# A first unit on the unnormed stream, and waits moved between the experts' passes

## The chip, the core and the metric

The kernel runs on one core of a Trainium2 chip. The metric is the device time of one execution in microseconds (us), as the median of the runs shown. The core has four engines that compute: TensorE (PE, with its weight loads PEld), VectorE (DVE), ScalarE (ACT) and GpSimd (POOL). SyncE (SP) only issues DMAs here. Each engine runs its own list of instructions in order; semaphores tie the lists together.

## The reference

Two transformer blocks are computed for 256 tokens of width 1024. The first puts 16 meta tokens ahead (272 rows in all) and begins like this:

```python
n = _rmsnorm(h, pre_mix_norm[l])
proj = jnp.einsum('btd,dn->btn', n, w_in[l])
qkv = jax.nn.silu(_causal_conv(jnp.concatenate([q, k, v], axis=-1), conv_w))
```

where `_rmsnorm` multiplies each row by its own factor `rsqrt(mean(x*x) + EPS)` and by a gain for each column. After that come a gated delta rule, an indexed attention, a gated merge, and a feed-forward layer. The second block has attention over a context, a Fourier branch, and a mixture of 16 experts in 4 groups:

```python
def expert_step(acc, xs):
    w1e, w3e, w2e, ge = xs
    y = (jax.nn.silu(t @ w1e) * (t @ w3e)) @ w2e
    return acc + ge[:, None] * y, None
```

A router picks one group and two experts in it for each token; the other gates are zero. The result is normed once more.

## The kernel before, in words

**Weights.** All weights come as one stream of 1 MB units, each 1024 x 256. A ring of six slots (`ring`) takes them in the order of use; SP issues a slot's next unit when PE has used the one in it. Activations lie transposed, as eight blocks of 128 columns by 272 or 256 tokens.

**Split units.** Most units are multiplied in three parts of reduced-precision fp32: ACT copies the unit rounded into `w_high` (`highs`, L1629), DVE subtracts that copy from the unit and leaves the rest in the slot itself as `ring_low` (`lows`, L2101), and PE adds high x high (L706), high x rest (L707) and low x high (L712). PE waits for `high_ready` at the start of a unit and for `low_ready` ahead of L712. A few units are plain fp32 (`tiles_of_unit`, L679): the very first, ("gk", 0), is one of them.

**The start.** SP fetches the stream into `qc`, then the small constants `sm`, then the ring. ACT squares the stream into `vc` (L1643), PE sums the squares with a matmul of ones (L759), ACT takes the root, DVE the reciprocal `rB` (L2082) and then `nT` = stream x gain x `rB` (L2114). Unit 0 multiplies `nT`. ACT rounds `nT` into `nT_high` (L1650), DVE leaves `nT_rest` (L2120); unit 1 and all later ones of this stage use these two.

**The convolution behind the first twelve units.** Each unit gives two tiles of 128 columns, one to a PSUM bank. For a tile ACT writes the first tap (L1663), DVE adds three more (L2134), ACT takes a sigmoid into `scr` (L1669), POOL multiplies. ACT's list puts the next `w_high` between the sigmoids of a unit's two tiles, and DVE's list puts the next `ring_low` behind the taps of both. ACT then squares finished tiles into `mod_rows` (L1659), and PE sums those (L771) behind every unit from the third on.

**The router.** The product of `h2` (eight blocks, made by DVE from the units of `wo2`) with 20 router columns is a group of fp32 matmuls (L1316); sums of squares (L1324) go to the same bank. Blocks 0 to 5 are multiplied halfway through the last unit of `wo2`, blocks 6 and 7 behind it.

**The experts.** A pass takes two experts, twelve units: eight for the hidden layer (`half_rows`, L1374, the two experts side by side in PE's columns), four for the way back. Eight passes cover 16 experts with up to 64 tokens each; a loop of extra passes, counted at run time (one here), takes what is over, with six units. Twelve more slots (`more`) hold expert weights beside the ring. In a pass PE first gathers tokens for a later pass in some cases (L1386), multiplies, adds the pass before into the accumulators (`scatter`, L1406, from `yb_high` and `yb_low`), turns the hidden rows (L1443), turns the choices and gates (L1447, L668), and multiplies back (L1374 on `hid`; L1418 in the extra pass). ACT empties the turned hidden rows (`hid`, L2040), then the turned choices (`spread`), then the gates (`gate_slot`, L2045); DVE leaves the low half of the output rows (`yb_low`, L2756). Behind the loop come the last `scatter`, the residual (L2866), the squares' sum (L1481) and the norm.

The order of the work is written out by hand; nothing plans it.

Of the kernel before, what the change touches and what calls it, by code (L numbers as in the profile page):

```python
# [9 lines left out]
KT = D // 128  # L10
META = 16
SEQ = 256
T = META + SEQ
# [114 lines left out]
STAGGER = 16  # L128
# [44 lines left out]
def build(nc, stream, h_in, ctx_in, c1_in, c2_in, sm_in, ws_in, wr_in, lam_in, out):  # L173
# [4 lines left out]
    with top:  # L178
# [52 lines left out]
        with ExitStack() as mixer:  # L231
# [33 lines left out]
            with ExitStack() as m:  # L265
# [74 lines left out]
        with ExitStack() as m:  # L340
# [25 lines left out]
            _under_merged2 = sb(m, "under_merged2", 128, 2 * KT * UNIT_COLS + 2 * KT * SEQ + STAGGER - 272 - used_words)  # L366
# [24 lines left out]
        h2tok_ready, h2tok_low_ready = sem("h2tok_ready"), sem("h2tok_low_ready")  # L391
# [84 lines left out]
        nT_rest_ready = sem("nT_rest_ready")  # L476
        cleared_ready = sem("cleared_ready")
# [38 lines left out]
        rexp_ready = sem("rexp_ready")  # L516
# [34 lines left out]

        CONV_TILES = [(kind, j) for kind in ("gk", "gq", "gv") for j in range(H)]
# [88 lines left out]
        def _(pe):  # L641
# [54 lines left out]
            def split_tiles(kind, u, high_x, low_x, n, names, k_ready=lambda k: None, halfway=lambda: None, drains=1):  # L696
# [4 lines left out]
                for k in range(KT):  # L701
                    k_ready(k)
                    for j in range(2):
# [69 lines left out]
            for t in range(0, 24, 2):  # L773
# [534 lines left out]
            def router_blocks(blocks):  # L1308
# [9 lines left out]
                if blocks[0] == 0:  # L1318
                    pe.wait_ge(partial_ready, 3)
                for k in blocks[-1:] if blocks[0] == 0 else blocks:  # L1320
# [16 lines left out]
            def between_wo2(u):  # L1337
# [3 lines left out]
                elif u == 3:  # L1341
                    router_blocks(range(6))

            pe.wait_ge(small_loaded, 32)
            for u in range(4):
                split_tiles("wo2", u, lambda k: merged2_high[:, k, :], lambda k: merged2_low[:, k, :], SEQ, [("wo2", u)],
                            lambda k: pe.wait_ge(merged2_ready, k // 2 + 1) if u == 0 else None, lambda: between_wo2(u), drains=0)
            router_blocks(range(6, KT))
            pe.wait_ge(h_ready, 3 * KT)
# [1687 lines left out]
```

## Time and profile before

| | |
|---|---|
| median of 3 runs | 1209.31 us (1208.77 to 1213.37) |
| the profiled execution | 1205.35 us, of which the span is 1203.2 us |
| PE busy | 1153.4 us, 96% of the span |
| DVE, ACT, POOL busy | 663.2, 499.2, 87.0 us |
| DMA | 254.59 MB, mean 212 GB/s; 420 to 422 GB/s through most of the experts' passes |

The page's engine rows tell how long each engine was busy; PE's ends are modelled, so a busy PE is not PE at its peak. What counts for an edit is the stage that it touches: which wait ends last there. The timeline lists instructions with the idle time ahead of each and what ended it; the chain of waits follows the end of the execution back to its start; the waits view sums who waited for whom.

### The profile page before, as it was taken

What the parts mean: (1) busy time and instruction counts of PE and PEld (TensorE: products, weight loads), DVE (VectorE), ACT (ScalarE), POOL (GpSimd) and SP (SyncE); (2) the same over time, 40 slices, a digit from 0 to 9 for tenths busy, and PEclk for the clock granted to TensorE, in tenths of its full rate; (3) what the DMA queues carried; (4) which work ended last, traced back from release to release, by engine and by line L of the source; (5) the groups of instructions that cost most, each with busy time, mean ns of one, the idle gap of its engine ahead of it and who ended that gap; (6) DMA issues with size and microseconds to landing.
All of it is one profiled execution on the core that took longest, in us unless ns stands there. A gap on an engine that the chain in (4) does not pass through costs nothing.

```text
span 1203.2 us, 21401 instructions
## 1 busy us (share of the span) xinstructions
PE 1153.4 (96%) x8936; PEld 996.9 (83%) x8936; DVE 663.2 (55%) x1143; ACT 499.2 (41%) x797; POOL 87.0 (7%) x92
## 2 busy tenths in 40 slices
PE   7999899999999989999999999999999899999996
PEld 6998789998979969999979889767899766665764
DVE  5777875588866476665555342775557531221223
ACT  5766523644374555544445222667344311111112
POOL 2451320000000100000100000000002000000000
PEclk9999999999999999999999999999999899999998
DMA  9544240443514746555564321302857899999980
GB/s 368 206 143 175 71 176 1 141 154 131 189 54 152 270 176 245 189 196 184 202 245 175 116 94 71 141 2 114 340 181 299 335 422 421 420 420 420 422 366 36
DMA packets 36204, 254.59 MB, mean 212 GB/s; under 512 B 4048, under 2 KB 4192, under 8 KB 5904
## 3 DMA queue, kind: packets, MB, share of 16 engines
q1 hardware_dynamic: 33552, 237.84, 51.4%
q0 software_dynamic: 2560, 15.42, 3.3%
q8 instruction: 71, 1.16, 0.4%
q14 instruction: 21, 0.17, 0.0%
HBM read 252.19 MB, written 1.05 MB: 210 GB/s over the span
## 4 chain that ended last, share of the span: by engine, by line
PE 85%; DVE 9%; ACT 3%; issue 2%; DMA 0%; DVEq 0%; ACTq 0%
PE bank L1374 13%; PE bank L712 12%; PE bank L706 12%; PE bank L707 12%; PE bank L668 5%; PE bank L1096 5%; PE bank L1182 4%; PE bank L1103 3%; PE bank L1386 2%; PE bank L759 2%; PE bank L1406 2%; PE bank L728 1%; PE bank L883 1%; DVE ring_low L2101 1%; PE bank L1284 1%
## 5 line engine op out<-in xcount | busy, mean ns | idle before, releaser
L2101 DVE TENSOR_TENSOR ring_low<-ring,w_high 128x2048 fp32r<-128x2048 f32 x104 | 238.0, 2290 | 160.8 <-ACT w_high L1629 160.7
L1629 ACT ACTIVATE w_high<-ring 128x2048 fp32r<-128x2048 f32 x104 | 199.1, 1915 | 281.5 <-PE bank L712 192.9
L706 PE MATMUL bank<-nT_high,w_high 128*128 128x256 f32 (+1 forms) x448 | 114.6, 295 | 0.0
L706 PEld LDWEIGHTS bank<-nT_high,w_high 128*128 128x128 f32 x448 | 84.2, 188 | 2.6 <-issue 2.4
L1374 PE MATMUL bank<-more,xs 128*64 128x256 f32 x768 | 84.6, 379 | 0.0
L1374 PEld LDWEIGHTS bank<-more,xs 128*64 128x64 f32 x768 | 58.7, 137 | 25.7 <-issue 2.2
L706 PE MATMUL bank<-hcl,w_high 128*128 128x256 f32 (+1 forms) x272 | 73.1, 306 | 0.0
L707 PE MATMUL bank<-hcl,w_high 128*128 128x256 f32 (+1 forms) x272 | 71.2, 299 | 0.0
L707 PE MATMUL bank<-nT_low,w_high 128*128 128x256 f32 (+1 forms) x272 | 64.7, 280 | 0.0
L706 PE MATMUL bank<-nMs,w_high 128*128 128x256 f32 x256 | 60.3, 280 | 1.4 <-DVE nMs L2493 1.4
L1096 PE MATMUL bank<-up,w_high 128*128 128x256 f32 x512 | 60.7, 276 | 0.0
L712 PE MATMUL bank<-nT_high,ring_low 128*128 128x256 f32 (+1 forms) x448 | 59.0, 284 | 0.5 <-DVE ring_low L2101 0.5
L707 PE MATMUL bank<-nMs,w_high 128*128 128x256 f32 x256 | 59.4, 276 | 0.0
L1096 PEld LDWEIGHTS bank<-up,w_high 128*128 128x128 f32 x512 | 59.3, 188 | 0.0
L712 PEld LDWEIGHTS bank<-nT_high,ring_low 128*128 128x128 f32 x448 | 55.8, 188 | 1.2 <-DVE ring_low L2101 0.7
L706 PEld LDWEIGHTS bank<-hcl,w_high 128*128 128x128 f32 x272 | 51.2, 188 | 4.1 <-issue 2.1
L707 PEld LDWEIGHTS bank<-hcl,w_high 128*128 128x128 f32 x272 | 51.2, 188 | 3.1 <-issue 1.0
L707 PEld LDWEIGHTS bank<-nT_low,w_high 128*128 128x128 f32 x272 | 51.2, 188 | 1.5 <-issue 1.4
L2756 DVE SCALAR_TENSOR_TENSOR yb_low<-bank,gate_slot,yb_high 128x512 fp32r<-128x512 f32 x18 | 13.5, 751 | 69.7 <-ACT yb_high L2049 69.7
L706 PEld LDWEIGHTS bank<-nMs,w_high 128*128 128x128 f32 x256 | 48.1, 188 | 3.0 <-issue 1.8
L707 PEld LDWEIGHTS bank<-nMs,w_high 128*128 128x128 f32 x256 | 48.1, 188 | 0.0
L707 PE MATMUL bank<-nT_rest,w_high 128*128 128x272 f32 x176 | 44.4, 288 | 0.0
(565 smaller groups left out, 2479.5 us busy)
## 6 DMA issues: line engine op xcount, KB each, us to landing
ring<-stream SPq DMA_DIRECT2D x163, 1024.0 KB, 4.9
more<-stream SPq DMA_DIRECT2D x60, 1024.0 KB, 18.7
more<-stream POOLq DMA_DIRECT2D x10, 1024.0 KB, 15.0
c<-constants_one SPq DMA_DIRECT2D x1, 1657.0 KB, 16.2
qc<-h_in SPq DMA_DIRECT2D x4, 272.0 KB, 3.8
c<-constants_two POOLq DMA_DIRECT2D x1, 1056.0 KB, 9.0
beside<-stream POOLq DMA_DIRECT2D x1, 1024.0 KB, 13.0
hT<-h_in POOLq DMA_DIRECT2D x1, 1024.0 KB, 6.0
```

The source lines that it names most:

```text
L668: last = nc.tensor.matmul(dst, lhs, rhs, start=(i == 0), stop=(i == len(pairs) - 1))
L706: nc.tensor.matmul(into[j], w, high_x(k), start=first, stop=False, skip_group_check=True)
L707: nc.tensor.matmul(into[j], w, low_x(k), start=False, stop=False, skip_group_check=True)
L712: last = nc.tensor.matmul(into[j], low_w[:, k, j * 128:(j + 1) * 128], high_x(k), start=False, stop=(k == KT - 1), skip_group_check=True)
L759: last = nc.tensor.matmul(psum[banks.at[name]][:, 0:n], ones, src[:, k, :], start=(k == 0), stop=(k == KT - 1), skip_group_check=True)
L1096: nc.tensor.matmul(dst[:, j * SEQ:(j + 1) * SEQ], high_w[:, k, j * 128:(j + 1) * 128], up[:, kg * KT + k, part, :], start=(kg == 0 and k = ...
L1103: last = nc.tensor.matmul(dst[:, j * SEQ:(j + 1) * SEQ], low_w[:, k, j * 128:(j + 1) * 128], up[:, kg * KT + k, 0, :], start=False, stop=( ...
L1182: return nc.tensor.matmul(dst[tp][:, j * 256:(j + 1) * 256], hcl[:, 2 * tp + part, k, j * 128:(j + 1) * 128], w[:, k, :], start=first, sto ...
L1374: last = nc.tensor.matmul(dst[rows, :], stationary[:, k, rows], w[j][:, k, :], start=(k == 0), stop=(k == n_k - 1))
L1386: last = nc.tensor.matmul(dst, part[:, qt, ft * 128:(ft + 1) * 128], pick[:, qt, 0:width], start=(qt == 0 and part is h2tok_high), stop=(q ...
L1629: A(w_high[:, d % 2, :], ring[:, s, :], ACT.Copy).then_inc(high_ready, 1)
L2101: TT(ring_low[:, s, :], ring[:, s, :], w_high[:, d % 2, :], sub).then_inc(low_ready, 1)
```

## The change

- **Start.** DVE multiplies the stream by the gain alone into `gained` (eight operations, in the room of `sums`) as soon as the stream has landed. Unit 0 multiplies `gained` instead of `nT`, so it needs no root. DVE multiplies its two output banks by `rB` in place, behind `nT_rest` and ahead of the first `ring_low`; ACT's first two taps wait for that. ACT makes the first `w_high` ahead of `nT_high`. Unit 1 waits for `nT_rest` block by block.
- **Router.** Blocks 0 to 5 are multiplied among the blocks of the last `wo2` unit; only the squares stay halfway.
- **Experts.** The first pass turns the choices ahead of the hidden rows. Every pass waits for `gate_slot` ahead of the second half of the way back, not of the first. `scatter` waits for each half of `yb_low` by itself. In an extra pass half of the `scatter` goes ahead of `half_rows` and half behind, and the wait for the gates goes down to where they are used.
- **Names and places.** One semaphore is shared to make room for the new one; `STAGGER` goes from 16 to 48 words, which moves buffers by 32 or more words.

```diff
-STAGGER = 16
+STAGGER = 48
...
+                _stagger_dsa = sb(m, "stagger_dsa", 128, STAGGER)
...
-            _under_merged2 = sb(m, "under_merged2", 128, 2 * KT * UNIT_COLS + 2 * KT * SEQ + STAGGER - 272 - used_words)
+            _under_merged2 = sb(m, "under_merged2", 128, 2 * KT * UNIT_COLS + 2 * KT * SEQ + STAGGER + 16 - 272 - used_words)
...
+        gained = sums[:, 0:H * T].rearrange("p (k n) -> p k n", n=T)
...
                 if t == 0:
-                    tiles_of_unit(kind, u, nT, T, names, k_ready=lambda k: pe.wait_ge(nT_ready, k + 1))
+                    tiles_of_unit(kind, u, gained, T, names, k_ready=lambda k: pe.wait_ge(gained_ready, k + 1))
                 else:
-                    if t == 2:
-                        pe.wait_ge(nT_rest_ready, KT)
-                    split_tiles(kind, u, lambda k: nT_high[:, k, :], lambda k: nT_rest[:, k, :], T, names)
+                    split_tiles(kind, u, lambda k: nT_high[:, k, :], lambda k: nT_rest[:, k, :], T, names,
+                                lambda k: pe.wait_ge(nT_rest_ready, k + 1) if t == 2 else None)
...
                 elif u == 3:
-                    router_blocks(range(6))
+                    router_squares([5])
+
+            def among_wo2(u, k):
+
+                blocks = {0: [0], 1: [1], 2: [2], 3: [3], 5: [4], 7: [5]}.get(k)
+                if u == 3 and blocks:
+                    router_blocks(blocks)
...
-            def scatter(count, signal=False, first=False):
-
-                pe.wait_ge(ys_ready, count * 2 + 2)
-                pe.wait_ge(spread_ready, count + 1)
-                for ft in range(KT):
+            def scatter(count, signal=False, first=False, fts=range(KT)):
+
+                if fts[0] == 0:
+                    pe.wait_ge(spread_ready, count + 1)
+                for ft in fts:
+                    if ft % 4 == 0:
+                        pe.wait_ge(ys_ready, count * 2 + 1 + ft // 4)
...
                     gather_blocks(range(KT), 2 * CAP)
-                    scatter(count - 1)
+                    scatter(count - 1, fts=range(4))
...
+                if first:
+                    turn_choices()
+                    turn_hidden()
+                else:
+                    scatter(count - 1, first=(n == 1), fts=range(KT) if n < PAIRS else range(4, KT))
+                    turn_hidden()
+                    turn_choices()
...
-                pe.wait_ge(gate_slot_ready, count * 2 + 2)
                 for q in range(2):
+                    if q == 1:
+                        pe.wait_ge(gate_slot_ready, count * 2 + 2)
...
             with pe.Fori(0, extra) as x:
-                pe.wait_ge(gates_loaded, 2 * x + 2)
                 expert_pass(PAIRS, x, x + PAIRS, lambda qt: gate_of[:, qt, :])
...
+            highs(1)
             for k in range(KT):
                 act.wait_ge(nT_ready, k + 1)
                 A(nT_high[:, k, :], nT[:, k, :], ACT.Copy).then_inc(nT_high_ready, 1)
-            highs(1)
...
             def tap(t):
                 kind, j = CONV_TILES[t]
+                if t < 2:
+                    act.wait_ge(gained_ready, KT + t + 1)
...
             dve.wait_ge(sm_loaded, 16)
+            for k in range(KT):
+                dve.wait_ge(h_loaded[k // 2], 16)
+                TS(gained[:, k, :], qc[:, k, :], small("g_pre_mix")[:, k:k + 1], None, mul).then_inc(gained_ready, 1)
             inv_rms("ss_in", T)
...
+            for t in range(2):
+                bank = full(dve, CONV_TILES[t])
+                TT(bank[:, 0:T], bank[:, 0:T], rB[:, 0:T], mul).then_inc(gained_ready, 1)
             lows(1)
```

DVE's list at the start of the program, before, from the reciprocal of the root to the first `ring_low`:

```order
L2082 RECIPROCAL rB<-root 128x272 [waits bank_free0,sm_loaded]
L2114 SCALAR_TENSOR_TENSOR nT<-qc,sm,rB 128x272 [waits dve_step]
L2114 SCALAR_TENSOR_TENSOR nT<-qc,sm,rB 128x272 x7
L2116 TENSOR_TENSOR silu_c<-sm,a 128x8x2 [waits sig_ready]
L2120 TENSOR_TENSOR nT_rest<-nT,nT_high 128x272 [waits nT_high_ready] x8
L2101 TENSOR_TENSOR ring_low<-ring,w_high 128x2048 [waits high_ready]
```

The same place after, where `sums` is the room of `gained` and `unit_used0` stands for the second tile of unit 0:

```order
L2146 TENSOR_SCALAR sums<-qc,sm 128x272 [waits h_loaded0,sm_loaded]
L2146 TENSOR_SCALAR sums<-qc,sm 128x272 [waits h_loaded0]
L2146 TENSOR_SCALAR sums<-qc,sm 128x272 [waits h_loaded1] x2
L2146 TENSOR_SCALAR sums<-qc,sm 128x272 [waits h_loaded2] x2
L2146 TENSOR_SCALAR sums<-qc,sm 128x272 [waits h_loaded3] x2
L2114 RECIPROCAL rB<-root 128x272 [waits bank_free0]
L2149 SCALAR_TENSOR_TENSOR nT<-qc,sm,rB 128x272 [waits dve_step]
L2149 SCALAR_TENSOR_TENSOR nT<-qc,sm,rB 128x272 x7
L2151 TENSOR_TENSOR silu_c<-sm,a 128x8x2 [waits sig_ready]
L2155 TENSOR_TENSOR nT_rest<-nT,nT_high 128x272 [waits nT_high_ready] x8
L2158 TENSOR_TENSOR bank<-bank,rB 128x272 [waits bank_full1]
L2158 TENSOR_TENSOR bank<-bank,rB 128x272 [waits unit_used0]
```

Eight operations stand ahead of the reciprocal now, and two on banks stand between `nT_rest` and the first `ring_low`, which comes next.

PE's list at the end of the eighth pass and the entry of the loop of extra passes, before (`more,hid` is the way back, `c` holds the identity, `plan` the count of extra passes, `pick` the gather):

```order
L1447 MATMUL bank<-c,pick_again 128x128 [waits again_ready]
L1447 MATMUL bank<-c,pick_again 128x128
L668 MATMUL bank<-c,pick_again 128x2 x2
L1374 MATMUL bank<-more,hid 64x512 [waits more_loaded2,more_loaded5,gate_slot_ready,hid_ready]
L1374 MATMUL bank<-more,hid 64x512 x7
L1374 MATMUL bank<-more,hid 64x512 [waits more_loaded7,more_loaded6]
L1374 MATMUL bank<-more,hid 64x512 x7
L634 TENSOR_LOAD plan [waits plan_ready]
L634 ISA x2
L1473 UNCONDITIONAL_BRANCH
L1473 ISA
L1434 ISA [waits gates_loaded]
```

The same place after, down to the first matmul of the gather:

```order
L1467 MATMUL bank<-c,pick_again 128x128 [waits again_ready]
L1467 MATMUL bank<-c,pick_again 128x128
L671 MATMUL bank<-c,pick_again 128x2 x2
L1388 MATMUL bank<-more,hid 64x512 [waits more_loaded5,more_loaded2,hid_ready]
L1388 MATMUL bank<-more,hid 64x512 x7
L1388 MATMUL bank<-more,hid 64x512 [waits more_loaded7,more_loaded6,gate_slot_ready]
L1388 MATMUL bank<-more,hid 64x512 x7
L637 TENSOR_LOAD plan [waits plan_ready]
L637 ISA x2
L1504 UNCONDITIONAL_BRANCH
L1504 ISA
L1400 MATMUL bank<-pick,c_rounded 128x128 [waits pick_ready]
```

The wait for `gate_slot_ready` went down by eight matmuls, and the wait for `gates_loaded` left the head of the loop.

## Rows read from the trace of the kernel before

**Rows 1.** The page: shares of the chain that ended last, by engine

```profile
PE 85%; DVE 9%; ACT 3%; issue 2%; DMA 0%; DVEq 0%; ACTq 0%
```

**Rows 2.** Timeline of the start: start us, length us, engine, line, operation, count, idle before

```profile
4.38 6.89 PE L759 MATMUL bank<-vc,ones 128*128 128x272 f32 x16 [4.38 <-ACT vc L1643]
...
14.44 8.96 PE L679 MATMUL bank<-nT,ring 128*128 128x272 f32 x32 [3.17 <-DVE nT L2114]
...
17.18 2.90 DVE L2120 TENSOR_TENSOR nT_rest<-nT,nT_high 128x272 fp32r<-128x272 f32 x8
...
20.00 2.29 DVE L2101 TENSOR_TENSOR ring_low<-ring,w_high 128x2048 fp32r<-128x2048 f32 x1
...
24.14 1.91 ACT L1629 ACTIVATE w_high<-ring 128x2048 fp32r<-128x2048 f32 x1
...
29.00 3.04 DVE L2134 SCALAR_TENSOR_TENSOR kc<-bank,sm,kc 128x271 f32<-128x271 f32 x6 [0.63 <-ACT kc L1663]
...
33.08 0.74 ACT L1659 ACTIVATE mod_rows<-kc 128x272 f32<-128x272 f32 x2
...
35.22 1.08 PE L771 MATMUL bank<-mod_rows,ones 128*128 128x272 f32 x4
```

**Rows 3.** One tile's instructions, `nT`: count, ns min/median/max, first and last start

```profile
L2114 DVE SCALAR_TENSOR_TENSOR nT<-qc,sm,rB x8: 497/498/502, 13.8 to 16.7; 128x272 f32<-128x272 f32 x8
```

**Rows 4.** DVE's groups by shape: count, busy us, mean ns, idle before

```profile
L2361 DVE TENSOR_TENSOR rot<-bank,c 128x272 f32<-128x272 f32 x3 | 1.3, 440 | 0.9 <-PE bank L978 0.8
```

**Rows 5.** DMA issues at 2.6 and 3.1 us: count, KB, us to landing

```profile
sm<-smalls SPq DMA_DIRECT2D x1, 127.0 KB, 4.7
ring<-stream SPq DMA_DIRECT2D x1, 1024.0 KB, 7.1
```

**Rows 6.** PE's timeline in the last unit of wo2

```profile
934.10 2.75 PE L1316 MATMUL bank<-wr,c 128*128 128x20 f32 x24
```

**Rows 7.** PE's waits after 900 us: total us, times, longest us

```profile
PE bank L1374 <- ACT hid L2040: 3.0, 4, 0.8
PE bank L1386 <- DVE gate_of L2858: 1.8, 1, 1.8
...
PE bank L1406 <- DVE yb_low L2756: 1.6, 1, 1.6
PE bank L1443 <- DVE hid_rows L2787: 1.4, 2, 0.9
...
PE bank L1418 <- ACT gate_slot L2045: 0.8, 1, 0.8
```

**Rows 8.** The chain in the experts' passes: start us, length us, what

```profile
969.59 0.22 PE bank L1447 x2
969.81 0.34 PE bank L668 x4
...
998.36 0.68 issue
...
1128.73 3.63 PE bank L1386 x32
...
1153.19 2.07 PE bank L1406 x16
...
1165.90 5.62 PE bank L1386 x32
...
1174.80 7.11 PE bank L1374 x64
```

**Rows 9.** DVE's timeline at its entry of the loop of extra passes

```profile
1155.20 0.15 DVE L2849 COPY shift<-c 128x1 f32 x1 [1.18 <-issue]
```

**Rows 10.** Busy us by PE, PEld, DVE, ACT, POOL, then granted clock, DMA share, GB/s

```profile
1170.00:1171.00 1.00, 1.00 (x7) 1.00 (x7) 0.00 (x0) 0.00 (x0) 0.00 (x0) 0.50 0.29 123
```

**Rows 11.** The DMA issued at 1121.3 us: count, KB, us to landing

```profile
more<-stream SPq DMA_DIRECT2D x1, 1024.0 KB, 26.1
```

**Rows 12.** PE's timeline in the eighth pass

```profile
1146.11 7.08 PE L1374 MATMUL bank<-more,xs 128*64 128x256 f32 x64
```

More of the change, by code:

```diff
@@ L702, in split_tiles @@
                     k_ready(k)
+                    among(k)
                     for j in range(2):
@@ L1317, in router_blocks, with router_squares @@
                                          start=(k == 0 and qt == 0), stop=False, skip_group_check=True)
-                if blocks[0] == 0:
-                    pe.wait_ge(partial_ready, 3)
-                for k in blocks[-1:] if blocks[0] == 0 else blocks:
+            def router_squares(blocks):
+                dst = psum[banks.at["router"]]
+                pe.wait_ge(partial_ready, 3)
+                for k in blocks:
                     if k >= 6:
@@ L1346, in _ @@
                 split_tiles("wo2", u, lambda k: merged2_high[:, k, :], lambda k: merged2_low[:, k, :], SEQ, [("wo2", u)],
-                            lambda k: pe.wait_ge(merged2_ready, k // 2 + 1) if u == 0 else None, lambda: between_wo2(u), drains=0)
+                            lambda k: pe.wait_ge(merged2_ready, k // 2 + 1) if u == 0 else None, lambda: between_wo2(u), drains=0,
+                            among=lambda k: among_wo2(u, k))
             router_blocks(range(6, KT))
+            router_squares(range(6, KT))
             pe.wait_ge(h_ready, 3 * KT)
@@ L1435, in expert_pass, with turn_hidden, turn_choices @@
                     gather_blocks(range(KT), 2 * CAP)
-                    scatter(count - 1)
+                    scatter(count - 1, fts=range(4))
                     for q in range(2):
                         half_rows(n, again, 2 * q, psum[q][:, 0:256], xs[:, :, 0:2 * CAP], KT, UNIT_COLS, rows_ready if q == 0 else lambda k: None)
-                if n < PAIRS and not first:
-                    scatter(count - 1, first=(n == 1))
-                pe.wait_ge(hid_rows_ready, count + 1)
-                for k in range(4 if n < PAIRS else 2):
-                    last = nc.tensor.transpose(psum[2][:, k * 128:(k + 1) * 128], hid_rows[:, k * 128:(k + 1) * 128], ident)
-                last.then_inc(hid_full, 1)
-                pe.wait_ge(again_ready, count * 4 + 4)
-                for qt in range(2):
-                    nc.tensor.transpose(psum[3][:, qt * 128:(qt + 1) * 128], pick_again[:, qt, :], ident)
-                group(psum[3][:, SEQ:SEQ + 2], [(pick_again[:, qt, :], gates(qt)) for qt in range(2)]).then_inc(spread_full, 1)
+                def turn_hidden():
+                    pe.wait_ge(hid_rows_ready, count + 1)
+                    for k in range(4 if n < PAIRS else 2):
+                        last = nc.tensor.transpose(psum[2][:, k * 128:(k + 1) * 128], hid_rows[:, k * 128:(k + 1) * 128], ident)
+                    last.then_inc(hid_full, 1)
+                def turn_choices():
+                    pe.wait_ge(again_ready, count * 4 + 4)
+                    for qt in range(2):
+                        nc.tensor.transpose(psum[3][:, qt * 128:(qt + 1) * 128], pick_again[:, qt, :], ident)
+                    if n == PAIRS:
+                        pe.wait_ge(gates_loaded, 2 * again + 2)
+                    group(psum[3][:, SEQ:SEQ + 2], [(pick_again[:, qt, :], gates(qt)) for qt in range(2)]).then_inc(spread_full, 1)
+                if first:
[5 more added lines that the diff above has]
+                    turn_choices()
                 if n == 0:
```

17 lines of the change are left out of this document (9 added, 8 removed).

## The prediction

> **What bounds the kernel now.** I read the chain by engine first: PE carries 85% of it, DVE 9%, DMA nothing [rows 1]. So a gain must be time in which PE stands still or runs slowly, and it counts only if nothing else ends late in its place. Then the timeline of the start: PE sums squares from 4.38 to 11.27, stands 3.17 us until the first `nT`, and multiplies unit 0 from 14.44 to 23.40 [rows 2]. Last PE's waits in the experts' part: four of about 0.75 us for `hid`, 1.8 us for the gates of the extra pass, 1.6 us for `yb_low`, 0.9 us for the first hidden rows, 0.8 us for `gate_slot` [rows 7]. The change goes at each of these. [...]
>
> **The start.** `gained` needs `sm`, which lands at 2.59 + 4.7 = 7.3 us, and slot 0, at 3.06 + 7.1 = 10.2 us [rows 5]. I price its eight operations at no more than 0.5 us each, by an operation of the same size with one more operand [rows 3]; that fills 4 us of DVE's idle time and is done by 11.3 us. So unit 0 starts at 11.3 instead of 14.44 and ends by 20.3 even at the old 8.96 us. That is 3.1 us on PE, but I don't take it, because what is late next is DVE and ACT. `nT_rest` still ends at 20.0 [rows 2]: the reciprocal and `nT` have not moved, and making `w_high` first costs `nT_high` nothing that DVE sees, since DVE's eight are the slower. Then come the two new operations on banks. No row shows DVE writing a bank; reading one at this size costs 0.44 us [rows 4], so I take 0.9 us for both, with ends of 0 (hidden) and 1.8 us (twice the row). Queued behind them on DVE: `ring_low`, the taps of the first tile, then ACT's sigmoid and its next `w_high`. That `w_high` ended at 24.14 + 1.91 = 26.05; now 26.95. PE gets there earlier: two units take 35.22 - 23.40 = 11.8 us, 5.9 each, so unit 1 ends by 26.2, and PE starts unit 2 at 27.0 instead of some 29.3. Then `ring_low` of unit 2 ends at 29.25, the taps behind it start there instead of at 29.00, so ACT's squares end at 33.08 + 0.74 + 0.25 = 34.07 instead of 33.82. PE, back from unit 2 at about 33, waits for them at L771: its second half goes at 34.2 instead of 35.22 + 0.5 = 35.7. From there DVE and ACT gain on PE in each unit, since in the trace they stand idle before every set of taps. So the start is worth **1.5 us**, and with the ends above 0.7 to 2.4. It barely hangs on how fast unit 0 runs. All that comes later starts from PE, and moves with it.
>
> **The router.** The same 24 matmul records of 128x20 move by some microseconds, from one block to six pieces. Together they take 2.75 us, 0.11 each, whatever their few columns [rows 6]; cut in six they hide at most partly behind wide matmuls. I take 0, with a loss of up to 0.6 (0.1 for each return) and a gain of as much. The wait behind the unit, for DVE's last `h2`, stays.
>
> **The passes.** In the first, the turned choices take 0.22 + 0.34 = 0.56 us [rows 8] and now lie within the 0.9 us that PE waits for the hidden rows: **0.56**. In passes two, four, six and eight PE starts the way back 0.68 us after `hid` is done [rows 8], because it waits for `gate_slot`, three operations further in ACT's list; I leave 0.09 for the signal, so 4 x 0.59 = **2.36**. The moved wait stands ahead of the second half, eight matmuls later, when ACT's short operations on the gates are over; what is queued behind it is that half alone. In the other passes a gather lies there already: 0.
>
> **The extra pass.** PE started the gather at 1165.90 [rows 8] after standing 1.8 us [rows 7], so it is done with the eighth pass at 1164.1. With the gates' wait gone, what remains is the entry of the loop: loading the count and a branch. No row shows it alone on PE. DVE stood 1.18 us at its own entry [rows 9], with one load more; the other end is 0, hidden while the last matmuls run. I take 0.6. [...]
>
> So: gather from 1164.7 at the full clock, 3.63 to 1168.3; half a `scatter`, 2.07 / 2 = 1.04 [rows 8], to 1169.4; `half_rows` 7.11 to 1176.5; the other half of `scatter`, 1.04, to 1177.5, half of it beside DVE's making of the hidden rows. The turn came at 1174.80 + 7.11 + 0.5 = 1182.4 before: **4.9 us**, of which 1.2 are the wait, 3.2 the clock and 0.5 the overlap. Then `gate_slot`, 0.8 less 0.1: **0.7**. At the last `scatter` PE waits 1.6 us for the second `yb_low`, while the first is done before the multiplication ends; half the `scatter`, **1.0**, goes into that. DVE's residual starts as much earlier, so the squares' sum is not held up.
>
> **Sum.** 1.5 + 0 + 0.56 + 2.36 + 4.9 + 0.7 + 1.0 = 11.0 us. The profiled execution took 1205.35 us and would take 1194.3; against the median, 1209.31 - 11.0 = **1198.3 us**. The ends of the unknown prices give 8 to 13.5 us, 1195.8 to 1201.3.
>
> **The rivals.**
>
> *The clock stays down in the extra pass.* If the loop's entry costs PE all of DVE's 1.18 us, the gap shrinks only from 1.8 to 1.2, and the granted clock may fall as before: 0.6 + 3.2 less, 7.2 us gained, 1202.1. For it: the fall behind the gap of 1.8. Against it: the gaps of 0.75 in four passes have no slow matmuls behind them. [...] Chance 0.15.
>
> *The stream of weights becomes the bound.* Through the passes the DMAs are full, whatever PE does. A unit for the last quarter of the eighth pass's hidden layer was issued at 1121.3 and landed 26.1 us later, at 1147.4 [rows 11]; PE takes it in the second half of the 7.08 us from 1146.11, at 1149.6 [rows 12]. So 2.2 us are left, and by then PE is 0.56 + 3 x 0.59 = 2.3 us ahead. It fits only just. If the stream lands later by some us, PE waits there, and the 2.9 us of the passes go: 8.1 gained, 1201.2. Chance 0.10.
>
> *The start gives nothing.* If the two bank operations cost several times the row, or PE's new short waits there (about 0.8 us at unit 2, 1.2 at L771) bring the lower clock, the 1.5 go: 1199.8. Chance 0.10.
>
> *Slower.* `STAGGER` moves buffers by 32 words or more. If PE read its operands more slowly at the new addresses, its whole share of the chain would stretch, 0.85 x 1203.2 = 1023 us [rows 1]. From 1.7% on that is 17.4 us, more than the 11 gained and the 6 that a measurement can tell: 1215.7. Against it: eight operations on rows of 272 words, at eight different offsets, agree within 497 to 502 ns [rows 3]. Chance 0.03.
>
> *It doesn't do what it says*: waits merely trade places and all lies within 6 us. Chance 0.02.
>
> **How the numbers follow.** The forecast has 0.60. Forecast, clock, stream and start are faster by over 0.5%, about what a measurement here can tell from no change (below 1203.3): 0.95 less some for two of them at once and for the spread of the runs, 0.88. Within it 0.09, slower 0.03. The range takes the forecast's own 1195.8 to 1201.3, the clock and the stream up to 1202.1, and two rivals together up to 1204.5; below, an us for the spread: 1194.5 to 1204.5.
>
> **What would show it.** Right: L679 begins at about 11.3, PE idles before unit 2, and L771's second half begins near 34.2; the way back in even-numbered passes starts 0.1 us after `hid`; the gather of the extra pass takes 3.6 us at granted clock 1.00 and `half_rows` starts 4.7 us after the eighth pass. Wrong: bank operations over 1 us each, a wait for a DMA in passes seven to nine, a granted clock of 0.50 behind the eighth pass, or longer steps between matmuls everywhere.

## The result and the profile after

The changed kernel takes 1190.03 us (median of four executions, 1189.76 to 1190.30), the kernel before 1210.34 us measured beside it (1208.77 to 1213.37). The ratio is 0.983, with a 95% interval of 0.981 to 0.985: 20.3 us gained, where 11.0 were forecast and 1194.5 us was the lower end of the range. The direction and every place at which the forecast saw a gain were right; the size was not. One execution of the experiment on the gates ran at a mean granted clock of 0.841 and took 1307.34 us; it is in no median below.

The profiled execution of the changed kernel took 1190.30 us, with a span of 1188.5 us at a mean granted clock of 0.995. The one of before took 1205.35 us, 1203.2 and 0.988. So the two traces show 15 us, and another 5 us lie between the profiled execution of before and its own median. Both parts need an explanation. (In all that follows a *fall* of the clock is a stretch at a granted clock of 0.50, the lowest in the 18 traces; outside the falls they show 1.00.)

First the timeline of the start (start, length, engine, line; L759 of before is L763 now, L679 is L682, L771 is L775), which answers to [rows 2]:

```profile
4.23 6.83 PE L763 MATMUL bank<-vc,ones 128*128 128x272 f32 x16 [4.23 <-ACT vc L1673]
6.93 2.26 DVE L2146 TENSOR_SCALAR sums<-qc,sm 128x272 f32<-128x272 f32 x8 [5.58 <-DMA sm<-smalls]
10.90 7.50 PE L682 MATMUL bank<-sums,ring 128*128 128x272 f32 x32
...
19.72 0.79 DVE L2158 TENSOR_TENSOR bank<-bank,rB 128x272 f32<-128x272 f32 x2
...
24.55 1.90 ACT L1659 ACTIVATE w_high<-ring 128x2048 fp32r<-128x2048 f32 x1
...
33.21 1.18 PE L775 MATMUL bank<-mod_rows,ones 128*128 128x272 f32 x4 [0.39 <-ACT mod_rows L1689]
```

PE goes from the squares' sum to unit 0 without standing still; `sums` is the tile that holds `gained`. Unit 0 takes 7.50 us instead of 8.96, DVE's two operations on the banks 0.79 us together. L775 begins 2.0 us before L771 did.

Then the same timeline in the extra pass: the end of the eighth pass's way back, the first two matmuls of the gather, its last, and the scatter and hidden rows behind it. It answers to [rows 8] and [rows 10].

```profile
1152.63 4.03 PE L1388 MATMUL bank<-more,hid 128*64 128x512 f32 x18
1156.59 0.33 PE L1400 MATMUL bank<-pick,c_rounded 128*128 128x128 f32 x1
1156.75 0.27 PE L1400 MATMUL bank<-pick,h2tok_low 128*128 128x128 f32 x1
...
1160.10 0.28 PE L1400 MATMUL bank<-pick,h2tok_low 128*128 128x128 f32 x1
1160.21 0.34 PE L1422 MATMUL bank<-spread,yb_high 128*128 128x256 f32 x1
...
1161.30 7.13 PE L1388 MATMUL bank<-more,xs 128*64 128x256 f32 x64
```

No gap is left: the way back ends at 1152.63 + 4.03 = 1156.66 and the gather has begun at 1156.59. It takes 1160.38 - 1156.59 = 3.8 us instead of 5.62, and the stretches around it have a granted clock of 1.00 (PE's busy time is the first pair of numbers, the clock the number before the DMA share):

```profile
core 0: us, PE busy (x) PEld busy (x) DVE busy (x) ACT busy (x) POOL busy (x), PEclk, DMA share, GB/s
141.00:144.00 3.00, 2.59 (x13) 2.33 (x14) 2.91 (x4) 0.63 (x3) 1.81 (x2) 1.00 0.89 295
144.00:147.00 3.00, 2.75 (x15) 2.15 (x14) 2.83 (x10) 0.28 (x1) 0.41 (x1) 1.00 0.45 188
165.00:168.00 3.00, 2.63 (x22) 2.62 (x23) 1.69 (x3) 1.11 (x2) 1.42 (x2) 1.00 1.02 431
168.00:171.00 3.00, 3.00 (x29) 3.00 (x28) 1.38 (x2) 0.68 (x2) 1.45 (x2) 1.00 1.03 437
1160.00:1170.00 10.00, 10.00 (x91) 7.32 (x90) 1.53 (x3) 0.57 (x2) 0.00 (x0) 1.00 0.26 109
...
```

In the trace of before two stretches between 140 and 175 us, which the forecast didn't look at, have a granted clock of 0.51 and 0.53:

```profile
144.00:147.00 3.00, 3.00 (x9) 2.38 (x8) 2.90 (x4) 0.00 (x0) 0.64 (x2) 0.51 0.80 311
168.00:171.00 3.00, 3.00 (x17) 3.00 (x16) 0.37 (x2) 1.10 (x2) 1.61 (x2) 0.53 1.02 431
```

Last, the waits of PE that answer to [rows 7] (engine, what it works on, who is waited for: total, times, longest). Those for `hid`, `gate_of` and `gate_slot` are gone, the one for `yb_low` fell from 1.6 to 0.4, the one for the hidden rows from 0.9 to 0.2; new are 1.6 and 0.4 us at the start.

```profile
PE bank L710 <- ACT w_high L1659: 1.6, 1, 1.6
PE bank L1422 <- DVE yb_low L2794: 0.4, 1, 0.4
PE bank L775 <- ACT mod_rows L1689: 0.4, 1, 0.4
PE bank L1460 <- DVE hid_rows L2825: 0.2, 1, 0.2
```

Where the 14.7 us between the two spans arise, by how much earlier the same line of PE starts in the trace of after:

| up to | gained so far | in this stage | forecast |
|---|---|---|---|
| end of the start (L771, L775 and on to 140 us) | 1.8 us | 1.8 | 1.5 |
| 200 us | 3.1 | 1.3 | no term |
| head of the experts' part, 940 us, the router with it | 4.2 | 1.1 | 0 |
| way back of the first pass | 4.9 | 0.7 | 0.56 |
| end of the eighth pass | 7.4 | 2.5 | 2.36 |
| turn in the extra pass | 13.1 | 5.7 | 4.9 |
| way back of the extra pass | 13.9 | 0.8 | 0.7 |
| end | 14.7 | 0.8 | 1.0 |

So the stages that the forecast named give 12.3 us against 11.0 in this pair of traces. What it had no term for is 2.4 us within the traces and 5 us outside them.

### The profile page after: what moved, and what is told of

Its sections match the earlier page's. It is cut to its first block, busy times and chain, and to the rows that moved or that the text cites. A ratio compares the mean times of both kernels' runs of the same rounds, so it can differ in the third digit from the quotient of the medians.

```text
span 1188.5 us, 21411 instructions
## 1 busy us (share of the span) xinstructions
PE 1145.3 (96%) x8936; PEld 981.5 (83%) x8936; DVE 665.7 (56%) x1153; ACT 497.4 (42%) x797; POOL 86.2 (7%) x92
## 4 chain that ended last, share of the span: by engine, by line
PE 85%; DVE 9%; ACT 3%; issue 2%; DVEq 0%; ACTq 0%
PE bank L1388 15%; PE bank L716 12%; PE bank L710 12%; PE bank L711 12%; PE bank L671 5%; PE bank L1099 5%; PE bank L1185 4%; PE bank L1106 3%; PE bank L1400 2%; PE bank L1422 1%; PE bank L732 1%; DVE ring_low L2133 1%; PE bank L886 1%; PE bank L763 1%; PE bank L1211 1%
## 5 line engine op out<-in xcount | busy, mean ns | idle before, releaser
L1388 PEld LDWEIGHTS bank<-more,xs 128*64 128x64 f32 x768 | 55.0, 137 | 29.3 <-issue 2.3
```

The lines of the kernel that those rows point to most:

```text
L1388: last = nc.tensor.matmul(dst[rows, :], stationary[:, k, rows], w[j][:, k, :], start=(k == 0), stop=(k == n_k - 1))
```

## The experiments

**Is before's median another kernel than its profile?** The kernel before, unchanged, was run again with a second trace, and so were the start alone, everything but the start, and the shift of the buffers alone. I had two theories of the missing part: the granted clock falls at other places in other executions (clock theory), or the matmuls run faster at the new addresses (address theory).

> The kernel before, unchanged. Its profiled execution took 1205.35 us at a mean granted clock of 0.988, its other executions 1208.77 to 1213.37 us. Clock theory: what differs between executions is how often and where the granted clock falls to half, since an idle stretch such as the ones at 141 to 144 and 165 to 168 us is followed by slow matmuls in some executions and not in others; so the times spread over 1205 to 1213 us again, a longer execution has a lower mean clock (about 0.98 at 1210 us), and a second trace shows falls at other places than 13.8, 144, 168, 942, 949 and 1167 us. Address theory (the shifted buffers speed up what follows): the mean clock is 0.988 whatever the time, and the falls lie where they lay.

Measured: 1209.76 us, ratio 1.000 (0.998 to 1.002). Neither theory held alone. Over this study the kernel before was executed 98 times beside the others, in four sets. At a mean clock of 0.987 there are 38 different times: 7 between 1204.4 and 1205.4 us, 31 between 1209.3 and 1212.1, and none between. So the same program at the same clock has two times, 3.9 us apart at the nearest and some 5 us by their middles, and besides, times go with the clock (1202.6 to 1203.3 us at 0.989 and 0.990, 1206.4 to 1208.0 for nearly all at 0.985). How many fall into the faster group changes: none of the 98 lies between 1208.0 and 1209.0 us, and below that lie 6 of 29, 10 of 23, 18 of 24 and 6 of 22 of the four sets, whose medians are 1210.16, 1209.33, 1207.33 and 1209.73 us. So a kernel is best read against the executions of before in its own set. The changed kernel was measured in one set only, ahead of these four, and a distance of 2 or 3 us between it and a kernel of another set tells little. The profiled execution of before belonged to the faster group, its median to the slower one. The second trace belongs to the slower, and shows what the difference is. These rows give the shortest, middle and longest duration in ns and the first and last start of one line's matmuls; first the kernel before as profiled, then its second trace:

```profile
L706 PE MATMUL bank<-nMs,w_high x256: 276/276/392, 438.3 to 528.3; 128*128 128x256 f32 x128
L1096 PE MATMUL bank<-up,w_high x512: 276/276/285, 530.4 to 616.6; 128*128 128x256 f32 x171
```

```profile
L706 PE MATMUL bank<-nMs,w_high x256: 277/279/392, 435.5 to 527.8; 128*128 128x256 f32 x128
L1096 PE MATMUL bank<-up,w_high x512: 279/279/284, 529.9 to 618.6; 128*128 128x256 f32 x171
```

The stretch over `nMs` takes 92.3 us instead of 90.0, that over `up` 88.7 instead of 86.2: 4.8 us. A profiled duration overlaps the next matmul and its end is modelled, so the firmer figure is the step, the time from the start of one of them to the start of the next: in the middle it is 118 ns instead of 113. Its mean, without pauses, is 117.8 to 118.4 ns in the second trace and 113.6 to 116.2 in the first, whether ACT, DVE, both or neither are busy. So the longer step doesn't come from those engines being busy. Below, 276 ns stands for the short step and 279 ns or more for the longer one.

**The shift alone.**

```diff
-STAGGER = 16
+STAGGER = 48
+                _stagger_dsa = sb(m, "stagger_dsa", 128, STAGGER)
-  ... 2 * KT * SEQ + STAGGER - 272 - used_words)
+  ... 2 * KT * SEQ + STAGGER + 16 - 272 - used_words)
```

> The kernel before with only the buffers moved, by 32 words and more. Address theory: 4 us or more of the gain that no term of the forecast covers, 1206 us or less beside 1210.3, and the gain grows evenly from 290 to 920 us. Clock and price theories: the same time as the kernel before within 2 us, and the same lengths of the matmuls between 290 and 920 us.

Measured: 1203.43 us, ratio 0.995 (0.993 to 0.997), 6.7 us at the median; its 12 executions lie between 1201.27 and 1205.46 us, in one group. Over `nMs` and `up` the matmuls take 276 ns, without exception in the five traces with 48 words in this place:

```profile
L1097 PE MATMUL bank<-up,w_high x512: 276/276/280, 527.9 to 613.8; 128*128 128x256 f32 x171
```

The change of constants that the forecast priced at nothing is, with the extra pass, the largest single term. Against the trace of before, which had the short step as well, it still gains 1.4 us between 290 and 940 us, most of it outside that stage: 0.9 us lie between 859 and 933 us, in the matmuls over `hcl` and their neighbours. This is most of the 1.1 us in the table's third row.

**The shift taken out of the changed kernel**, the same edit backwards:

> The changed kernel with the addresses of the kernel before. Address theory: the matmuls over nMs and up between 438 and 616 us go back to some 279 to 280 ns instead of 276 in most executions, 1500 of them by 3 ns, and the median is 4.7 to 6.7 us above the changed kernel, 1194.7 to 1196.7 us, with some executions at 1190 to 1191 us at the same mean clock. Clock theory: the addresses do nothing in a kernel whose clock falls only twice, 1190 to 1191 us throughout.

Measured: 1195.40 us, ratio 0.990 (0.988 to 0.992), so 5.4 us above the changed kernel, and spread over 1193.37 to 1198.35 again. Its trace fell on the shortest of them, with 276 ns. The clock theory, 1190 to 1191 us throughout, fell. Of the eight traces with the old addresses four have the short step and four the longer one, each in both stretches.

**Which filler?** Only the first one is enlarged, so that `nMs`, `up` and the mixer's buffers move against the weights:

```diff
-        _stagger = sb(dense, "stagger", 128, STAGGER)
+        _stagger = sb(dense, "stagger", 128, 48)
-  ... 2 * KT * SEQ + STAGGER - 272 - used_words)
+  ... 2 * KT * SEQ + 48 - 272 - used_words)
```

> The kernel before, where only the first filler (behind the high parts of the weights) grows from 16 to 48 words; the second and third stay, so nMs, up and the mixer's buffers lie as in the changed kernel relative to the weights, and the buffers behind the other fillers don't. If the relative place of nMs and up is the cause: 1203.4 us beside 1210.2, and 276 ns between 438 and 616 us. If it is one of the other buffers: 1210 us.

Measured: 1206.27 us, ratio 0.998 (0.996 to 0.9995), with 276 ns over `up`. So this filler brings the fast step, as its trace shows. It doesn't bring the whole gain: 3.1 us beside its own runs of before, 6.7 with all fillers. In its trace unit 0 ran at a granted clock of 0.50 from 13 to 20 us, so part of the rest is that. Another part comes with the other fillers: between 859 and 933 us this kernel gains 0.1 us on the trace of before, the one with all fillers 0.9. What more they bring stays open. All these edits move many buffers at once, so they show that places matter, not which operand of a matmul it is.

**Other places.** The changed kernel with fillers of 32, 64, 80, 112 and 40 words; the only edit is the constant, `STAGGER = 32` and so on.

> The changed kernel with fillers of 32 words instead of 48. If each place but the old one is as good (a single unlucky address): 1190 us and 276 ns. If the old place and its neighbours share the loss: 1194.7 us or more, and 279 ns or more between 438 and 616 us.

> The changed kernel with fillers of 64 words. So far 32 words gave 281 ns between 438 and 616 us and 1199.9 us, 16 words 276 in some executions and 280 in others, 48 words 276. If the pattern repeats every 32 words, 64 is like 32: 281 ns and about 1200 us. If it is a matter of distance (further is better): 276 ns and 1190 us or less.

> The changed kernel with fillers of 80 words. Pattern of 32 words: like 16 and 48, 276 ns, 1190 to 1195 us. Distance: 276 ns and no more than 1190 us. If 48 is a lucky place alone: 279 ns or more and 1195 us or more.

> The changed kernel with fillers of 112 words. If the places repeat every 32 words and 16, 48 and 80 are of one kind: 276 or 280 ns by execution, 1190 to 1196 us, and not the 281 ns and 1200 us of 32 and 64. If they repeat every 64 words: like 48, 276 ns and 1190 us in each execution.

> The changed kernel with fillers of 40 words, between the slow 32 and the fast 48. If the time goes gradually with the place: 278 to 279 ns and some 1195 us. If what counts is a block of 16 words that a buffer begins in: as slow as 32, 281 ns and 1200 us, or as fast as 48, 276 ns and 1190 us.

| words | median us | executions | ratio to before (95%) | middle duration over `up` in the trace |
|---|---|---|---|---|
| 16 | 1195.40 | 1193.37 to 1198.35 | 0.990 (0.988 to 0.992) | 276 ns |
| 32 | 1199.91 | 1198.14 to 1200.71 | 0.992 (0.990 to 0.994) | 281 |
| 40 | 1203.29 | 1201.47 to 1204.11 | 0.994 (0.993 to 0.996) | 280 |
| 48 | 1190.03 | 1189.76 to 1190.30 | 0.983 (0.981 to 0.985) | 276 |
| 64 | 1203.32 | 1201.22 to 1205.57 | 0.996 (0.994 to 0.998) | 283 |
| 80 | 1193.71 | 1191.86 to 1198.40 | 0.988 (0.985 to 0.991) | 279 |
| 112 | 1191.36 | 1189.80 to 1193.16 | 0.985 (0.982 to 0.989) | 276 |

The row of 32 words, then that of 64, in the same view as above:

```profile
L1099 PE MATMUL bank<-up,w_high x512: 274/281/287, 530.6 to 619.6; 128*128 128x256 f32 x171
```

```profile
L1099 PE MATMUL bank<-up,w_high x512: 274/283/283, 534.9 to 624.7; 128*128 128x256 f32 x171
```

The step goes with the duration: 113 ns in the middle for 276 ns, 117 to 120 ns for the longer ones. There are three kinds of places. 48 and 112 words had the short step in every trace. 16 words has either step, and so has 80 by its times: at one mean clock, 0.994, two of its executions took 1193.38 and 1197.56 us. 32, 40 and 64 words are the slowest, each in one trace with the longer step. So 48 is not a lucky place alone, more distance is not better, and the time doesn't pass gradually from 32 to 48 (40 is slower than 32, for a reason not found). The seven places would fit a pattern that repeats every 64 words, with 32, 40 and 64 bad; seven places don't prove one. The stage between 859 and 933 us has the same order: against the changed kernel 112 words lose nothing there, 16 and 80 lose 0.8 and 0.9 us, 32, 40 and 64 lose 1.6, 1.8 and 2.1, by one trace each. With 64 words the change of addresses gives away 13 of the 20 us. What the spread of 16 and 80 comes from at unchanged addresses isn't settled: no row of the traces differs ahead of the stage in which the steps do.

**The start.** First alone on the kernel before (its core, the rest as in the change):

```diff
-                    tiles_of_unit(kind, u, nT, T, ... nT_ready ...)
+                    tiles_of_unit(kind, u, gained, T, ... gained_ready ...)
+            for t in range(2):
+                bank = full(dve, CONV_TILES[t])
+                TT(bank[:, 0:T], bank[:, 0:T], rB[:, 0:T], mul)
```

> Only the start of the change: unit 0 on the stream times the gain, the banks scaled by the root, the high parts of the second weight unit first. Price theory (the step of 1.5 us as forecast, 1.8 in the traces): 1208.5 to 1209 us beside 1210.3, and the two falls of the clock near 144 and 168 us stay. Clock theory: a start without the 3.2 us idle stretch also moves the falls near 144 and 168 us, so 3 to 8 us are gained, 1202 to 1207 us, with a mean clock above that of the kernel before. Address theory: 1.8 us and no more.

Measured: 1208.08 us, ratio 0.998 (0.996 to 0.9998), 2.1 us at the median. Its two falls of the clock lie at 140 to 144 and 164 to 168 us, so a better start doesn't remove them. On the time and on these falls the price theory is right. But the mean clock is above before's, as the clock theory had it: 0.987 to 0.991, where before's executions of the same set have 0.983 to 0.989.

Then the change without its start:

> The changed kernel with the start of the kernel before. Price theory: 1190.0 + 1.8 = 1191.8 us. Clock theory: 3 to 8 us more than the changed kernel, 1193 to 1198 us, with falls of the clock back near 144 and 168 us, at half the clock for some 3 us each. Address theory: 1191.8 us, and the falls near 144 and 168 us absent, as in the changed kernel.

Measured: 1193.82 us, ratio 0.986 (0.983 to 0.989), 3.8 us above the changed kernel. None of the three fits: the time is the clock theory's, but there is no fall near 144 or 168 us. Its trace says why it is more than 1.8: the squares' sum, the wait and unit 0, with the clock at 0.50 from 14 to 21 us.

```profile
4.57 6.86 PE L761 MATMUL bank<-vc,ones 128*128 128x272 f32 x16 [4.57 <-ACT vc L1672]
14.61 10.63 PE L680 MATMUL bank<-nT,ring 128*128 128x272 f32 x32 [3.17 <-DVE nT L2143]
```

Unit 0 takes 10.63 us here, 8.96 in the first trace of before and 7.57 in the second. In four of seven traces with the old start the clock fell in unit 0, in three it didn't; in none of the nine with the new start did it fall there. That raised the question what the clock alone is worth there. I filled the wait with matmuls whose sums nothing uses:

```diff
                 if t == 0:
+                    for _ in range(12):
+                        nc.tensor.matmul(psum[banks.turn % 8][:, 0:T], ones, vc[:, 0, :], start=True, stop=True)
                     tiles_of_unit(kind, u, nT, T, names, ...
```

> The kernel before with twelve more matmuls of 128x272 in the 3.2 us in which PE waits for the first nT; their sums are overwritten by unit 0 and used by nothing. If the start's gain beyond the forecast is the clock's (a fall to half in unit 0 in some executions, 0 to 3.6 us): unit 0 takes 7.5 us in the trace, none of the clock's falls lies before 30 us, and the median is 1 to 3 us lower than the kernel before. If the clock doesn't matter there: the same time within 0.5 us, or longer by what the twelve stick out.

Measured: 1205.96 us, ratio 0.998 (0.996 to 1.001): inconclusive. One matmul leaves two records here (the twelve are x24 in the timeline), so the filling took 5.66 us and unit 0 began at 16.14, more than 2 us after it could have. With six (`range(6)`):

> The kernel before with six more matmuls of 128x272 in the wait for the first nT, 12 records of 0.235 us, 2.8 us, so that they don't stick out as the twelve before them did (24 records, 5.66 us, 2.4 us too long). Clock theory of the start: unit 0 begins some 3.2 us after the squares' sum as before and takes 7.5 us in the trace, and the median is 0.5 to 3 us below the kernel before. If the start's gain is the earlier beginning alone: the same time within 0.5 us.

Measured: 1209.84 us, ratio 1.000 (0.998 to 1.002).

```profile
4.38 5.48 PE L759 MATMUL bank<-vc,ones 128*128 128x272 f32 x16 [4.38 <-ACT vc L1645]
9.70 2.91 PE L779 MATMUL bank<-vc,ones 128*128 128x272 f32 x12
13.03 7.57 PE L679 MATMUL bank<-nT,ring 128*128 128x272 f32 x32 [0.42 <-DVE nT L2116]
```

Unit 0 takes 7.57 us at a granted clock of 1.00, as in the twelve-fold filling (7.50 us, 1.00), and the median doesn't move by more than the interval of 2 to 3 us. So the fall in unit 0 is real where it happens, but it isn't what separates the median of before from its profile.

What the start gains the traces show better. These rows are the matmuls over `beside`, the next ones behind the convolution (first and last start at the end), in the first trace of before, in its second, and in the trace of the start alone:

```profile
L668 PE MATMUL bank<-beside,nT x48: 398/399/399, 96.3 to 107.4; 128*128 128x280 f32 x48
```

```profile
L668 PE MATMUL bank<-beside,nT x48: 398/399/399, 93.5 to 104.6; 128*128 128x280 f32 x48
```

```profile
L670 PE MATMUL bank<-beside,nT x48: 398/399/399, 92.9 to 103.9; 128*128 128x280 f32 x48
```

The squares' sum ends between 9.5 and 11.4 us in the traces, so I count from its end to the first of these matmuls: 83.3 to 83.4 us in the nine traces with the new start, 83.7 to 83.8 in the three with the old start and no fall in unit 0, and 85.0 to 86.9 in the four with the fall. The earlier beginning is therefore worth 0.2 to 0.5 us by itself, because DVE and ACT are late next; the rest of what the start gains is the fall that no longer happens. The kernel with six matmuls has no fall there either and comes to 83.7 us, so it should gain nearly as much, and its median doesn't show it. Whether before's executions fall in unit 0 as often as its traces isn't shown; for the median the interval of the start alone allows 0.2 to 5.2 us.

**The gates of the extra pass.** The wait moved, on the kernel before, and nothing else:

```diff
-                pe.wait_ge(gates_loaded, 2 * x + 2)
                 expert_pass(PAIRS, x, x + PAIRS, ...)
 ... in expert_pass, behind the turned choices:
+                if n == PAIRS:
+                    pe.wait_ge(gates_loaded, 2 * again + 2)
```

> The kernel before, where only the wait for the gates of the extra pass moves behind the turned choices. Forecast's step: 1.2 us of wait and 3.2 us of clock, 4.4 us gained; with a loop entry that costs nothing 5.0, so 1205.2 to 1205.8 us beside 1210.2; the gather at 3.6 us and full clock. Rival (the clock stays down behind the eighth pass whatever the wait): 0.6 to 1.8 us gained, 1208.4 to 1209.6 us, the gather at 5.6 us again.

Measured: 1202.74 us, ratio 0.9955 (0.9935 to 0.997), 6.6 us at the median. Against the trace of before PE is 4.6 us late at the end of the eighth pass (this trace has the longer step over `nMs` and `up`) and 0.5 us early behind the extra pass's multiplication: 5.1 us gained there, where 4.4 to 5.0 were expected. Here are the gather's rows of before, of this kernel and of the changed kernel with the wait put back (count, busy us and mean ns, then idle time before them), each from the stretch of 1148 to 1176 us:

```profile
L1386 PE MATMUL bank<-pick,c_rounded 128*128 128x128 f32 x16 | 5.3, 354 | 1.8 <-DVE gate_of L2858 1.8
```

```profile
L1386 PE MATMUL bank<-pick,c_rounded 128*128 128x128 f32 x16 | 3.7, 277 | 0.0
```

```profile
L1400 PE MATMUL bank<-pick,c_rounded 128*128 128x128 f32 x16 | 5.2, 348 | 1.8 <-DVE gate_of L2895 1.8
```

The last one is this experiment, the move undone in the changed kernel:

```diff
-                    if n == PAIRS:
-                        pe.wait_ge(gates_loaded, 2 * again + 2)
 ...
+                pe.wait_ge(gates_loaded, 2 * x + 2)
                 expert_pass(PAIRS, x, x + PAIRS, ...)
```

> The changed kernel with the wait for the gates back at the head of the extra pass. If the gap brings the clock's fall: 1.8 us of wait and some 3.2 us of clock come back, 1195.0 us beside 1190.0, and the gather takes 5.6 us. If the fall of the kernel before came from its earlier gaps: 1.8 us alone, 1191.8 us, and the gather takes 3.7 us.

Measured: 1196.18 us, ratio 0.989 (0.9855 to 0.993), 6.2 us above the changed kernel, 5.1 of them in the extra pass by the traces. The clock falls again behind a gap of 1.8 us:

```profile
1158.00:1161.00 3.00, 1.22 (x6) 0.14 (x2) 0.99 (x5) 0.69 (x1) 0.00 (x0) 1.00 1.00 423
1161.00:1164.00 3.00, 2.95 (x21) 2.96 (x22) 1.24 (x5) 0.00 (x0) 0.00 (x0) 0.80 0.99 418
1164.00:1167.00 3.00, 3.00 (x15) 3.00 (x16) 0.41 (x1) 0.00 (x0) 0.00 (x0) 0.50 0.36 153
```

So the wait cost 1.8 us and its clock 3.3, in both directions of the edit, by one trace each. The fall itself stands behind the eighth pass in all eight traces with the wait at the head of the extra pass, and in none of the ten without it.

**The experts' part alone**, on the start and the addresses of before:

> The kernel before with the experts' part of the change alone (first pass, way back, extra pass, last scatter), addresses and start as before. Forecast's terms: 0.56 + 2.36 + 4.9 + 0.7 + 1.0 = 9.5 us, with a loop entry of 0 us instead of 0.6 some 10.1; 1199.5 to 1200.5 us beside 1210. In the trace the matmuls over nMs and up take 276 ns or 280, as in the kernel before. If the gain of the experts hangs on the addresses or the start as well: under 8 us, 1202 us or more.

Measured: 1196.67 us, ratio 0.991 (0.987 to 0.994), 10.7 us at the median. In its trace PE is 2.2 us late behind the router (the granted clock was 0.50 there from 938 to 948.2 and from 951.8 to 955 us, in the trace of before from 942.2 to 945.7 and from 949.2 to 952.5), and the span ends 8.2 us earlier (1195.0 against 1203.2): 10.4 us, where the terms gave 9.5 to 10.1. The gain of the experts hangs neither on the start nor on the addresses. The three parts measured alone, 2.1, 6.7 and 10.7 us, add up to 19.5 of the 20.3 us; the router's part was not measured alone.

## Why the forecast was wrong

**The start, 1.5 us: right in its steps, lucky in its size.** `gained` was ready in time, unit 0 began at 10.90 (11.3 forecast), the bank operations took 0.40 us each (0.44 by [rows 4]), ACT's `w_high` ended at 26.45 (26.95), and L775's second half went at 33.21 + 1.18 / 2 = 33.8 (34.2). PE's new wait at unit 2 is 1.6 us instead of 0.8, because unit 0 was faster than assumed; what was late next was ACT, as said. 1.8 us came of it. But the sentence "It barely hangs on how fast unit 0 runs" holds for the changed kernel only. In the kernel before L706 starts at 23.0 us or at 20.2, according to the clock in unit 0, and the trace that the forecast was read from had a granted clock of 0.50 from 13.8 to 17.2 us, in part of it. Without that fall the same steps give 0.2 to 0.5 us, with a longer one more than 3.

**The router, 0: right.** The distance between the two traces is 4.3 us ahead of it and 4.2 to 4.3 behind it.

**The passes, 0.56 + 2.36: right**, 0.7 and 2.5. In the even passes PE starts the way back at 1149.57, after ACT's `hid` of 1148.92 and 0.60 us, so 0.05 us behind it; `gate_slot`, until 1150.10, is no longer waited for.

```profile
1148.92 0.60 ACT L2072 ACTIVATE hid<-bank 128x512 f32<-128x512 f32 x1 [8.78 <-PE bank L1460]
1149.48 0.39 ACT L2074 ACTIVATE spread<-bank 128x256 fp32r<-128x256 f32 x1
1149.76 0.34 ACT L2077 ACTIVATE gate_slot<-bank 64x1 f32<-64x1 f32 x2
```

**The extra pass, 4.9 + 0.7 + 1.0: right but for the loop's entry.** The 0.6 us for it were an estimate between DVE's 1.18 us [rows 9] and 0; no row of before shows PE's entry alone. In the trace of after the gather begins at 1156.59 us and the way back ends at 1156.66: PE's entry costs nothing that shows, so 5.7 us came instead of 4.9. The end of the range was the right value. The 3.2 us of clock in the 4.9 are 2.0 us of the gather and 1.2 of the `scatter` behind it, by [rows 8], at the clock of [rows 10]; the two traces of the experiment on the gates' wait put back give 3.3.

**The shift of the buffers, no term: this is the step that failed.** The forecast named `STAGGER` as the one way to a slower kernel, at 0.03, and argued from DVE's rows [rows 3] that addresses don't matter. DVE's rows say nothing about PE's operands. The rows that would have spoken are those of PE itself: matmuls of the same shape have means of 276 to 289 ns in the trace of before, from one pair of operands to another. No row says how much of that is the place, and the forecast didn't ask. Places have a price, and of either sign: 48 words take 5 to 7 us off at the median, 32 or 64 would have added 4.5 to 8. The gain and the loss were both on offer, so the right entry was a term of its own with wide ends, not a rival on one side.

**The base, 1205.35 against 1209.31 us.** The forecast took 11.0 us off the median as if the 4 us between profile and median lay outside the change. By the second trace they lay in the stage between 438 and 616 us, in executions with the longer step (4.8 us), and the shift ended them. The arithmetic: 15.05 us between the two profiled executions, 5.0 between profile and median of before, 0.3 of after, 20.3 in all.

**The clock between 140 and 175 us, no term.** 1.3 us in the pair of traces. Of the 18 traces of this study 11 show at least one of these falls, among them some with the new start and addresses, without a pattern that I could find; that the change removes them isn't shown.

**The rivals.** *The clock stays down*: it didn't; without the gap there is no fall behind the eighth pass in ten traces of ten, and with a gap of 1.8 us there is one, down to 0.50, in eight of eight, in both kernels. *The stream of weights*: no wait for a DMA appears in the passes. *The start gives nothing*: 2.1 us alone, 3.8 when taken out, and its bank operations took 0.40 us each. *Slower by the addresses*: steps do differ by the addresses, with the other sign at 48 words (113 ns in the middle over `up`, 118 in the second trace of before).

No version beat the changed kernel: 112 words come to 1191.36 us, and the two ranges of times overlap.

## What to carry to other kernels

A constant that only moves buffers is a change of its own: give it a term, try a few values, and read the steps of equal matmuls over different operands. Know whether the trace that a term is read from met a fall of the clock there: a term is worth what it ends in most executions, not in that one. If the profiled execution lies away from the median, find out which stage the difference is in before subtracting anything from the median. A wait ahead of matmuls costs more than its length where the granted clock falls behind it (here 1.8 us of wait and 3.3 us at 0.50), and such a wait is best moved behind work that doesn't need it.

## What the runs showed of the hardware

- Matmuls of 128x256 over `nMs` and `up` take 276 ns or 279 to 283 ns, by where the buffers lie: middle steps of 113 ns, or 117 to 120 ns. The good fillers were 48 and 112 words (and, in part of the executions, 16 and 80), the bad ones 32, 40 and 64. The longer step is there whether ACT and DVE are busy or not (117.8 to 118.4 ns on average in the second trace of before).
- At 16 words the same addresses give both steps, one through a whole trace (four traces of eight with each), and the kernel before has two groups of times some 5 us apart at one mean clock (0.987). Why is not known.
- A gap of 1.8 us ahead of the gather was followed by a granted clock of 0.50 in eight traces of eight, gaps of 0.75 us in the passes weren't. PE's entry into a loop cost 0 us right behind 16 matmuls (way back until 1156.66 us, gather from 1156.59).
- DVE multiplied a bank of 128x272 in place in 0.40 us.
